# An encoder trunk in fp32: attention with the keys on the partitions, and a state scan of three operations a step

## The reference, cut to what matters

```python
def one_block(qblk):
    s = jnp.einsum('bgrqd,bgkd->bgrqk', qblk, kt).astype(jnp.float32) * scale
    p = jax.nn.softmax(s, axis=-1).astype(vt.dtype)
    return jnp.einsum('bgrqk,bgkd->bgrqd', p, vt)
...
y_a = block_attention(q, k, v) * jax.nn.silu(gate_a)
...
_, states = lax.associative_scan(_linear_combine, (a_seq, bu), axis=1, reverse=reverse)
```

## Time and profile before

| | us |
|---|---|
| median of 3 runs | 2812.23 (2809.74 to 2815.75) |
| profiled execution | 2818.78 |
| its span | 2816.7 |
| of it, from `heads`' first scan step to `s5_outputs`' first instruction | 548.9 to 905.5 |

### The profile page before, as it was taken

The page is one execution under the profiler, slowest core; times in us unless marked ns, Lnnn a source line. Parts: engine busy times, 40 slices in busy tenths (PEclk is TensorE's granted clock), DMA queues, the critical chain, the costliest instruction groups (busy, mean ns, idle before and its releaser), DMA issues. The chain is left out here.

```text
span 2816.7 us, 41316 instructions
## 1 busy us (share of the span) xinstructions
PE 2561.4 (91%) x15638; PEld 2209.2 (78%) x15638; DVE 1419.5 (50%) x2285; ACT 924.0 (33%) x1916; POOL 1134.4 (40%) x1244
## 2 busy tenths in 40 slices
PE   6999997699998777899799999899899689999798
PEld 5988887589997666677588888777777579999687
DVE  6564444687887945322654453455555422222314
ACT  4232222633333233233322223356566400000331
POOL 3444441177776125412054554433333345553320
PEclk9999999999999888999899999999999799999899
DMA  7323333301111355444333333443423454442553
GB/s 162 114 61 106 106 106 82 64 24 47 32 39 31 61 108 169 144 166 147 116 100 129 117 145 126 133 164 107 167 96 130 174 169 145 147 145 90 172 172 149
DMA packets 268744, 328.33 MB, mean 117 GB/s; under 512 B 45684, under 2 KB 217358, under 8 KB 267414
## 3 DMA queue, kind: packets, MB, share of 16 engines
q1 hardware_dynamic: 230390, 239.10, 28.8%
q10 hardware_dynamic: 38176, 86.78, 8.3%
HBM read 212.75 MB, written 103.55 MB: 112 GB/s over the span
## 5 line engine op out<-in xcount | busy, mean ns | idle before, releaser
L1044 POOL TENSOR_TENSOR w_hi<-w_raw,ones 128x512 fp32r<-128x512 f32 (+1 forms) x232 | 277.2, 1195 | 771.3 <-PE r L1055 263.9
L1046 POOL TENSOR_TENSOR w_lo<-w_raw,w_hi 128x512 fp32r<-128x512 f32 (+1 forms) x232 | 342.0, 1474 | 18.2
L1055 PE MATMUL r<-h_lo,w_hi 128*128 128x264 f32 (+1 forms) x864 | 286.7, 332 | 0.0
L1055 PE MATMUL r<-h_hi,w_lo 128*128 128x264 f32 (+1 forms) x864 | 278.6, 322 | 0.0
L1055 PE MATMUL r<-h_hi,w_hi 128*128 128x264 f32 (+1 forms) x864 | 277.7, 321 | 0.0
L1055 PE MATMUL r<-xc_lo,w_hi 128*128 128x264 f32 (+1 forms) x768 | 248.8, 324 | 30.4 <-POOL w_lo L1046 30.4
L1055 PE MATMUL r<-xc_hi,w_lo 128*128 128x264 f32 (+1 forms) x768 | 249.4, 325 | 0.0
L1055 PE MATMUL r<-xc_hi,w_hi 128*128 128x264 f32 (+1 forms) x768 | 248.8, 324 | 0.0
L440 POOL TENSOR_TENSOR w_lo<-w_raw,w_hi 128x512 fp32r<-128x512 f32 x64 | 87.1, 1388 | 232.3 <-ACT w_hi L516 232.1
L1055 PEld LDWEIGHTS r<-xc_lo,w_hi 128*128 128x128 f32 x768 | 146.4, 191 | 43.1 <-issue 31.0
L1055 PEld LDWEIGHTS r<-h_lo,w_hi 128*128 128x128 f32 x864 | 163.0, 189 | 16.3 <-issue 2.4
(11 more groups left out here) (345 smaller groups left out, 6393.8 us busy)
## 6 DMA issues: line engine op xcount, KB each, us to landing
w_raw<-in_w_in_even SPq DMA_DIRECT2D x72, 256.0 KB, 3.0
w_raw<-in_w_in_odd SPq DMA_DIRECT2D x64, 256.0 KB, 3.5
w_raw<-in_w_ogate SPq DMA_DIRECT2D x64, 256.0 KB, 7.1
v_d<-vs ACTq DMA_DIRECT2D x8, 1152.0 KB, 4.2
us<-u_d SPq DMA_DIRECT2D x128, 65.0 KB, 3.1
xc_d<-xc ACTq DMA_DIRECT2D x8, 1040.0 KB, 6.5
qk_d<-qk ACTq DMA_DIRECT2D x16, 520.0 KB, 2.7
sz_d<-sz SPq DMA_DIRECT2D x8, 1040.0 KB, 5.2
```

The lines of the kernel that those rows point to most:

```text
L1044: self.nc.gpsimd.tensor_tensor(hi, raw, one, ALU.mult).then_inc(self.hi_done, 1)
L1046: self.nc.gpsimd.tensor_tensor(lo, raw, hi.bitcast(F32), ALU.subtract).then_inc(self.split, 1)
L1055: ins = self.nc.tensor.matmul(bank[:, 0:n], w[:, u % self.buffers, k, :], z[:, off:off + n], start=(first and k == 0 and w is self.hi and ...
```

## The change

`heads` keeps its job and its place. A head is now cut into two units, of 580 and 460 queries (PARTS; n counts 16 units), and its keys into nine blocks of 116 (the last 112; KEYS). Scores are made with a block of keys as stationary operand and the unit's queries as moving one, so that the keys lie on the partitions and no transposition of probabilities is needed. ACT copies each block of scores to SBUF (`keep`). DVE keeps a running maximum in `top`, from PSUM and from itself, once ACT has copied the block (`higher`), eight to a unit. `turn_top` transposes it, `find` reduces it to one maximum a query, `spread` transposes that back over all partitions, `lower` subtracts it from each block, `power` takes the exponential. `mix` has the probabilities stationary and v moving, with a 129th column of ones that gives the sum; ACT copies (`take_rows`), DVE inverts the sum, ACT scales (`scale_rows`), PE transposes the rows back (`turn_rows`), DVE gates (`out`). Unit n's scores stand beside the lowering of unit n-1 and the mixing of unit n-2. SP, not ACT, stores the result, in place of the gate. The scan's four operations become three: one multiplication of 128x256 (now times four factors, `step`), and two additions of 128x128 into the next Z.

```diff
-QT = [(0, 120), (120, 120), (240, 112), (352, 120), (472, 112), (584, 112),
-      (696, 120), (816, 112), (928, 112)]
+KEYS = [(i * 116, min(116, L - i * 116)) for i in range(NT)]
+PARTS = [(0, 580, 5, 116), (580, 460, 4, 115)]
+START = (222, 0)
+HALVES = ([(0, 290), (290, 290)], [(0, 460)])
+TOPS = ([0, 116, 232, 512, 628], [0, 116, 232, 348])
+TOP_RUNS = ([(0, 0, 3), (512, 3, 5)], [(0, 0, 4)])
+SPREAD_AT = (164, 0)
...
-    with do.loop(CH // 2, 8) as i:
+    with do.loop(CH // 2, 6) as i:
         for b in range(2):
-            now = t["Z"][:, bass.ds(i * 2 + b, 1), :, :].rearrange("p k q g -> p (k q) g")
+            now = t["Z"][:, bass.ds(i * 2 + b, 1), :, :]
             nxt = t["Z"][:, bass.ds(i * 2 + (b + 1), 1), :, :].rearrange("p k q g -> p (k q) g")
 
             gp.sem_inc(turns, 1)
-            do.free(tt(tmp[:, 0], now, t["step_re"][:, :, :], ALU.mult))
-            do(tt(tmp[:, 1], now, t["step_im"][:, :, :], ALU.mult))
-            do(tt(tmp[:, 0], tmp[:, 0], tmp[:, 1, ::-1, :], ALU.add))
+            do(tt(tmp[:, :, :, :], now.broadcast_to([P, 2, 2, G]),
+                  t["step"][:, :, :].rearrange("p (o q) g -> p o q g", o=2), ALU.mult))
+            do(tt(nxt, nxt, tmp[:, :, 0, :], ALU.add))
             gp.sem_inc(turns, 1)
-            do(tt(nxt, nxt, tmp[:, 0], ALU.add))
-
+            do(tt(nxt, nxt, tmp[:, :, 1, :], ALU.add))
...
-                    m = TILES[t1 - 1][1]
+                    m = KEYS[t1 - 1][1]
                     act.wait_ge(v_turned, 3 * n + part + 1)
-                    nc.scalar.activation(vt[0:m, t0:t1, n * HD:(n + 1) * HD],
+                    nc.scalar.activation(vt[0:m, t0:t1, n, 0:HD],
...
+    spot = [(n, i) for n in range(NU) for i in range(PARTS[n % 2][2])]
+    mixed_at, turned_at, out_at, turned_in = {}, {}, {}, [0] * (LAST + 2)
+    for w, (n, i) in enumerate(spot):
+        at = (n + 2) * NT + (NT * (i + 1) - 1) // PARTS[n % 2][2]
+        mixed_at.setdefault(at, []).append(w)
+        at += 2
+        while at % NT in (0, NT - 1):
+            at += 1
+        turned_at.setdefault(at, []).append(w)
+        out_at.setdefault(at + 1, []).append(w)
+        for later in range(at // NT, LAST + 2):
+            turned_in[later] = w + 1
+    LOWERED = {0: ((2, 8),), 3: ((1, 0),), 4: ((1, 1), (1, 2)), 5: ((1, 3),), 6: ((1, 4), (1, 5)), 7: ((1, 6),),
+               8: ((1, 7),)}
...
+        sb = s.sb("prob", [P, NB, NT, WIDE])
+        top, peak = s.sb("top", [P, WIDE]), s.sb("peak", [P, 5])
+        o_raw, o_row, inv = s.sb("o_raw", [P, 2, HD + 1]), s.sb("o_row", [P, 3, HD]), s.sb("inv", [P, 4])
...
+        def region(n, k):
+            return reg[n % 2][(11 * (n // 2) + k) % 2]
...
+                def scores(n, j):
+                    off, width, tiles, m = PARTS[n % 2]
+                    ko, kn = KEYS[j]
+                    g = n // 2 % KV
+                    if j == 0:
+                        pe.wait_ge(q_done, n + 1)
+                        if n >= 2:
+                            pe.wait_ge(found, n - 1)
+                        if n and turned_in[n - 1]:
+                            pe.wait_ge(yd, turned_in[n - 1])
+                    elif j == 1:
+                        if n >= 2:
+                            pe.wait_ge(low, NT * (n - 1))
+                    else:
+                        pe.wait_ge(kept, NT * n + j - 1)
+                        pe.wait_ge(raised, (NT - 1) * n + j - 2)
+                    out = region(n, j)
+                    for o, w in HALVES[n % 2]:
                         for x, z in ((0, 1), (0, 0), (1, 0)):
+                            last = nc.tensor.matmul(out[0:kn, START[n % 2] + o:START[n % 2] + o + w],
+                                                    kr[z][:, g, ko:ko + kn], q[x][:, off + o:off + o + w],
+                                                    start=(z == 1), stop=(x == 1))
+                    last.then_inc(sc, 1)
...
+                def turn_top(n):
+                    off, width, tiles, m = PARTS[n % 2]
+                    pe.wait_ge(kept, NT * n + 8)
+                    pe.wait_ge(raised, (NT - 1) * (n + 1))
...
+                    for i in range(tiles):
+                        at = TOPS[n % 2][i]
+                        last = nc.tensor.transpose(out[0:m, at:at + KEYS[0][1]], top[0:KEYS[0][1], i * m:(i + 1) * m],
+                                                   c["ident"][0:KEYS[0][1], 0:KEYS[0][1]])
+                    last.then_inc(tt, 1)
...
+                def spread(n):
+                    off, width, tiles, m = PARTS[n % 2]
+                    pe.wait_ge(found, n + 1)
+                    pe.wait_ge(kept, NT * (n + 1))
...
+                        last = nc.tensor.transpose(out[0:KEYS[0][1], at:at + m],
+                                                   peak[0:m, i:i + 1].broadcast_to([m, KEYS[0][1]]),
+                                                   c["ident"][0:m, 0:m])
+                    last.then_inc(sp_done, 1)
...
+                def mix(n, j):
+                    off, width, tiles, m = PARTS[n % 2]
+                    g = n // 2 % KV
+                    for x in range(j * tiles, (j + 1) * tiles):
+                        i, k = divmod(x, NT)
+                        w = DONE[n] + i
+                        if i == 0:
+                            pe.wait_ge(ex, NT * n + k + 1)
+                        if k == 0 and w >= 2:
+                            pe.wait_ge(taken, w - 1)
+                        kn = KEYS[k][1]
+                        last = nc.tensor.matmul(o_slot(w)[0:m, :], sb[0:kn, n % NB, k, i * m:(i + 1) * m],
+                                                vt[0:kn, k, g, :], start=(k == 0), stop=(k == NT - 1))
+                        if k == NT - 1:
+                            last.then_inc(pv, 1)
...
+                def turn_rows(w, n):
+                    m = PARTS[spot[w][0] % 2][3]
+                    if n <= NU:
+                        pe.wait_ge(found, n)
+                    pe.wait_ge(scaled, w + 1)
+                    if w:
+                        pe.wait_ge(yd, w)
+                    nc.tensor.transpose(region(n - 1, NT)[:, 0:m], o_row[0:m, w % 3, :],
+                                        c["ident"][0:m, 0:m]).then_inc(tu, 1)
+                pe.wait_ge(ones_set, 1)
+                for n in range(LAST + 1):
+                    for j in range(NT):
+                        if n < NU:
+                            scores(n, j)
+                        if j == 2 and 1 <= n <= NU:
+                            spread(n - 1)
+                        if 2 <= n < LAST:
+                            mix(n - 2, j)
+                        for w in turned_at.get(n * NT + j, ()):
+                            turn_rows(w, n)
+                        if j == 0 and 1 <= n <= NU:
+                            turn_top(n - 1)
...
+                def keep(n, j):
+                    kn, width = KEYS[j][1], PARTS[n % 2][1]
+                    if j == 0 and n >= NB:
+                        act.wait_ge(pv, DONE[n - NB + 1])
+                    act.wait_ge(sc, NT * n + j + 1)
+                    nc.scalar.activation(sb[0:kn, n % NB, j, 0:width],
+                                         region(n, j)[0:kn, START[n % 2]:START[n % 2] + width],
+                                         ACT.Copy).then_inc(kept, 1)
+                def power(n, j):
+                    kn, width = KEYS[j][1], PARTS[n % 2][1]
+                    act.wait_ge(low, NT * n + j + 1)
+                    nc.scalar.activation(sb[0:kn, n % NB, j, 0:width], sb[0:kn, n % NB, j, 0:width], ACT.Exp,
+                                         scale=SCALE).then_inc(ex, 1)
...
+                def take_rows(w):
+                    m = PARTS[spot[w][0] % 2][3]
+                    act.wait_ge(pv, w + 1)
+                    nc.scalar.activation(o_raw[0:m, w % 2, :], o_slot(w)[0:m, :], ACT.Copy).then_inc(taken, 1)
+                def scale_rows(w):
+                    m = PARTS[spot[w][0] % 2][3]
+                    act.wait_ge(got, w + 1)
+                    if w >= 3:
+                        act.wait_ge(tu, w - 2)
+                    nc.scalar.activation(o_row[0:m, w % 3, :], o_raw[0:m, w % 2, 0:HD], ACT.Copy,
+                                         scale=inv[0:m, w % 4:w % 4 + 1]).then_inc(scaled, 1)
...
+                for n in range(LAST + 1):
+                    for j in range(NT):
+                        for w in mixed_at.get(n * NT + j - 1, ()):
+                            take_rows(w)
+                        if n < NU:
+                            keep(n, j)
+                        for back, k in LOWERED.get(j, ()):
+                            if 0 <= n - back < NU:
+                                power(n - back, k)
+                        for w in mixed_at.get(n * NT + j - 1, ()):
+                            scale_rows(w)
+                        if j == 4 and n + 1 < NU:
+                            leading(n + 1)
...
+                def rest(n):
```

(71 more changed lines are left out.)

214 lines of the change are left out of this document (64 added, 150 removed).

## The result

The changed kernel takes 2777.79 us (median of 4 runs, 2775.85 to 2779.18) against 2811.06 for the kernel before beside it (4 runs, 2809.74 to 2815.75): a ratio of 0.9874, 95% interval 0.9859 to 0.989, 33.3 us less. The forecast was 2770, with 2758 to 2800 as its range.

The account below looks back on a forecast made before the run. PE was taken to bound attention, which ends the stage, with POOL's scan close behind. Heads of 36.2 us (33.4 + 1.8 + 1.0) and the scan both ended near 860; `s5_outputs` at 863 gave 2812.2 - 42.5 = 2770 us, range 2758 to 2800.

Parts of the forecast that it names:

- The ends, and which is last: Stage end: attention and scan both fall on 860, so `s5_outputs` was put at 863, 42.5 us earlier.
- the forecast's own band: Whole kernel: a time of 2764 to 2782 us, given chance 0.50.
- PE's own work: PE in a head: scores, `mix` and transposes sum to 33.4 us against 42.4 before.
- The scores: PE's score products: 9 x 1.39 = 12.5 us a head; a block 0.78 us for 580 queries, 0.61 for 460.
- The waits: PE waits 1.8 us a head at block 1's second `turn_rows`, 1.0 where DVE falls behind in 460 units.
- Beginning and end: Attention's ends: first `q_lo` at 554.0, units 0 and 1 27.5 us, units 16, 17 and last rows 22.5.
- The scan: POOL's scan: two steps in 4.66 to 4.86 us, 305 us plus 5 lost beside `rest`, ending at 859.
- (a): Rival, both ends: little wait, PE at 34 us a head, scan at its lower bound; 2760 us, chance 0.12.
- (c): Rival, DVE: PSUM reads cost more, 460 units are DVE's; 1.2 us more a unit, 2783 us, chance 0.06.
- (d): Rival, POOL: `higher` and `lower` block it, 75 us; scan ends at 934, time 2841 us, chance 0.07.
- (b): Rival, handoffs: PE waits in most blocks, 40 us a head, 2797 us; chance 0.25 together with (e).
- (e): Rival, `keep`: it reads each block first, `higher` waits, so slow ACT sets the pace; chance 0.25 together with (b).

Follow-up runs that it names:

- both moves: Changed kernel with the second `turn_rows` of a block moved to the next block without one, and the q split at blocks 1 and 2, not 4 and 5: 2765.68 us.
- without a scan: Changed kernel with both moves and the scan left out: 2757.12 us (one run).
- short maximum: Changed kernel with both moves, no scan, and the running maximum from block 2 on over 116 columns only, exponent scaled by a further 1/100: 2750.66 us (one run).
- 116 keys: Kernel before with its keys in tiles of 116, the last of 112, instead of 128 and 16: 2801.61 us, ratio 0.9961.
- rows apart: Changed kernel with the second `turn_rows` of a block moved to the next block without one: 2771.64 us, ratio 0.9853 to the kernel before.
- early split: Changed kernel with the split of q (`leading`, `rest`) at blocks 1 and 2 instead of 4 and 5: 2765.55 us, ratio 0.9834 to the kernel before.
- flat scan: Changed kernel with both moves and the scan's 130 steps written out, without loop or semaphore counting the turns: 2757.38 us, ratio 0.9808 to the kernel before.

## Why the prediction was right

**The ends, and which is last.** Right in its mechanism. Put against the stage, the forecast was 314.1 us (356.6 less 42.5) and 321.0 was measured; 2770 and 6.9 are 2777, within 1 us of the time that came out. It stayed in the range, but near the upper edge (2782) of the forecast's own band. Attention alone was to need 311.6 us up to `s5_outputs` and needed 321.0, 9.4 more: 7.4 in seven heads, 2.6 in the first two and the last two units, less 0.6 in the tail. Which end would be last the forecast didn't say: it had both at 860 and added 2.5 us for that. The scan came where it was put (310.8 us long, 310 forecast) and attention did not, so these 2.5 us, meant for a race that didn't take place, made the miss smaller by luck.

**A head: PE's own work is the term that was mis-sized.** 33.4 us were forecast, and with both moves, then also without a scan, then with a short maximum too it is 34.31, 34.25 and 34.16: the forecast was 0.8 to 0.9 short, seven times. The scores did it. 12.5 us were forecast, from 1.39 a row of before. In the changed kernel, one key block of each kind, PE in order of time (a `mix` matmul leaves two records):

```profile
768.34 0.39 PE L1710 MATMUL long<-q_hi,k_lo 128*116 128x290 f32 x1 [0.21 <-DVE prob L1872]
768.57 0.30 PE L1710 MATMUL long<-q_hi,k_hi 128*116 128x290 f32 x1
...
769.24 0.39 PE L1749 MATMUL o<-v,prob 116*116 116x129 f32 x2
```

```profile
759.36 0.45 PE L1710 MATMUL short<-q_hi,k_lo 128*116 128x460 f32 x1
...
760.07 0.38 PE L1749 MATMUL o<-v,prob 116*115 116x129 f32 x2
```

That is 0.90 (0.88 elsewhere, without the wait's tail) and 0.71 where 0.78 and 0.61 were forecast, 1.6 a pair and 14.3 a head. Two things are in it. The first product of a block takes 0.23 up to the next one, the others 0.13 to 0.14: 0.09 more. (Here it stands behind fp32 matmuls; in unit 0, where it stands behind a short wait and no fp32 matmul, it takes 0.19 to 0.20. What causes it no run tells.) Before, this came once in a row of 1040 columns, now it comes twice, 0.8 a head. The other 1.1 or so is in the reading: in the kernel before, the row's products and what follows them are

```profile
702.28 0.38 PE L1655 MATMUL scores<-k_lo,q_hi 128*112 128x264 f32 x1
702.49 0.28 PE L1655 MATMUL scores<-k_hi,q_hi 128*112 128x264 f32 x1
...
703.79 1.09 PE L1666 MATMUL turned<-ident,prob 120*128 120x120 f32 x9
```

1.51 from matmul to matmul. The forecast took the weight loads, and the load of the first transpose runs 0.12 ahead of its matmul, under the last product. The row's sum was right, its division wrong, and the scores are the term that stayed while the others were replaced. `mix` and the transposes make up for half of it: 20.0 us against 20.9, `mix` records 0.10 to 0.11 apart where 0.112 was taken. The choice of the row of `s5_outputs` over the 0.132 of the kernel before was right, for the reason given: the 16-key tile, as the run with tiles of 116 shows.

**The waits** were right in size: 1.8 and 1.0 forecast, 1.63 and 1.31 by their removal. The place and cause of the first are as forecast. The second is in the 460 unit, as said, but it is three waits. At the longest, 0.7 us a head, the late engine was ACT, not DVE; the other two, 0.4 on `higher` and 0.2 on `lower`, are DVE's, the engine that the forecast had named. The working counted ACT by the unit ("under 15 in either") and dropped it; in block 4 ACT has a `keep`, two `power` and `leading` in a row, with the rows' copy queued behind. A sum over a unit can't show that; the order of the queue there can. So the price of this wait came out in part for a wrong reason, and that is luck.

**Beginning and end.** Together they turned out 2.6 over. In the last two units PE waits 3.9 us on ACT and DVE, which the forecast gave as "its waits" without a price. The beginning came out close by luck: the granted clock was 0.79 over the first 16.4 us of the stage (546.6 to 563), so at half for 7 us of them and not for the 14 of the forecast, but it fell again in unit 1, for 10 us, which wasn't forecast (last section).

**The scan.** 305 + 5 forecast, 306.8 + 4 measured; two steps 4.72 within 4.66 to 4.86, with the gap ahead of the first addition at 0.19, near the 0.17 of the cheaper case. That `rest` alone would still cost POOL anything is borne out too (the sixteen stretched operations above). Of the 24 us lost before 17 go with the product.

**Rivals.** (a) and (c) don't hold: PE waited, and an operation with an operand in PSUM took 757 ns where 0.76 was taken. (The 2783 of (c) doesn't follow from its 1.2 us: in eight units of 460 that is 9.6 us, 2780.) (d) is refuted: DVE's `higher` and `lower` run all through the scan, and the means of POOL's operations are 741 (L815), 471 (L817) and 469 ns (L819) against 0.73 and 0.45 to 0.46 us in the steps shown above, which nothing disturbs; what the means have over these is the sixteen operations beside `rest`. The Trainium skill, "SBUF — State Buffer", section "Who interferes with whom", has it that a DVE instruction with at most one SBUF input, outside the 2-port perf modes, leaves GpSimd alone. The trace now agrees for operations of 0.76 us too. The exception, which the prediction left out, matters for the product: it has one tensor in SBUF as input and yet held POOL (17 us with it); whether a 2-port mode is the reason, no run here shows. (b) and (e) happened in part: the waits cost 2.9 us a head, as much as the forecast had (2.8), and not 3.8 more.

**That whichever end is late counts** is what the experiments bear out most plainly: each improvement of one job alone (116 keys, rows apart, early split, flat scan) gave what was left until the other's end, and no more.

## What to carry to other kernels

When two jobs share a stage, work out both ends before pricing either: here attention that ended 21.5 us earlier showed as 12, and 19 us of scan as nothing. Price waits in an in-order queue by the block, not by the unit: an engine that is 70% busy was late at the longest of its waits, for a step placed in its fullest block and a copy queued behind it. Once the waits of one job are gone, look at the loop around the other: written out, the scan went from 2.36 to 1.89 us a step with the same three operations.

## What the runs showed of the hardware that was not expected

**Loop overhead on POOL.** Around three dependent operations, register loop, computed wait values and addresses, and semaphore increments leave gaps of 0.19, 0.18 and 0.18 or 0.50 us; written out they are 0.07 to 0.08. That is 60 us over 130 steps, more than the fourth operation cost (14 to 19). The run took all of these away at once, so what each costs isn't shown.

**A small last tile in fp32.** `mix` with its ninth stationary tile at 16 rows instead of 112 costs 0.37 us a row (4.71 against 4.34). The moving columns are the same. The time is lost on the way into the tile and out of it (0.30 and 0.29 us between loads instead of 0.11), not in it; why, no run here tells.

**The clock in the first units.** Granted clock (third number from the end) in the changed kernel:

```profile
563.00:572.00 9.00, 5.89 (x32) 3.97 (x30) 6.45 (x11) 5.63 (x9) 6.33 (x12) 1.00 0.06 21
572.00:582.40 10.40, 8.19 (x28) 6.60 (x29) 7.39 (x12) 7.65 (x14) 7.36 (x14) 0.51 0.12 30
```

Then the low stretch with both moves and no scan, and with the short maximum besides:

```profile
573.00:580.00 7.00, 5.88 (x17) 4.29 (x18) 6.52 (x11) 6.11 (x11) 0.00 (x0) 0.52 0.00 0
```

```profile
571.00:574.50 3.50, 3.12 (x8) 2.22 (x9) 3.15 (x7) 3.41 (x7) 0.00 (x0) 0.51 0.00 0
```

In unit 1 PE waits for DVE a third of the time, and then it runs at 0.51, about 1.2 GHz, for 10 us; ten records of `mix` take 2.14 us there (579.87 to 582.01) instead of 1.1. The drop comes in all three runs: with both moves and no scan it lasts 7 us, with less of DVE's work besides 3.5. None of them tells what makes it end. The kernel before, whose PE had work throughout (11.3 of the 12 us from 563 on, clock 0.95), had no such drop after its first 14 us. The forecast counted only the first stretch at half clock.
